# Gate and up of each feed-forward as seven block products instead of eight, with tokens on partitions

## What is computed

```python
def rmsnorm(x, w):                      # over the 1024 features
    return x * rsqrt(mean(x * x, -1) + 1e-6) * w

for l in range(2):
    x = x + 0.5 * (silu(rmsnorm(x, n1) @ w_gate) * (rmsnorm(x, n1) @ w_up)) @ w_down    # feed-forward 0, 2
    x = x + mixed(rmsnorm(x, nm) @ w_in) @ w_out
    x = x + 0.5 * (silu(rmsnorm(x, n2) @ w_gate) * (rmsnorm(x, n2) @ w_up)) @ w_down    # feed-forward 1, 3
x = x + mixed_2(rmsnorm(rmsnorm(x, nf), nm2) @ w_in_2) @ w_o_2
x = x + (silu(rmsnorm(x, n3) @ w_gate_2) * (rmsnorm(x, n3) @ w_up_2)) @ w_down_2        # feed-forward 4
return rmsnorm(x, nf2)
```

## Time and profile before

| | |
|---|---|
| median of 3 runs | 2558.16 us (2556.64 to 2558.29) |
| span of the profiled execution | 2554.3 us; its own time is not among the runs' |
| TensorE busy | 2518.2 us, 11986 matmuls |
| VectorE busy | 1324.1 us |
| ScalarE busy | 567.3 us |
| GpSimd busy | 1519.9 us |
| DMA | 228.67 MB, mean 90 GB/s |
| a feed-forward (1 and 2) | 359.95 and 359.94 us |
| the second block's mixer | 267.72 us |

### The profile page before, as it was taken

The page is one execution under the profiler, slowest core; times in us unless marked ns, Lnnn a source line. Parts: engine busy times, 40 slices in busy tenths (PEclk is TensorE's granted clock), DMA queues, the critical chain, the costliest instruction groups (busy, mean ns, idle before and its releaser), DMA issues.

```text
span 2554.3 us, 33028 instructions
## 1 busy us (share of the span) xinstructions
PE 2518.2 (99%) x11986; PEld 2058.2 (81%) x11986; DVE 1324.1 (52%) x1556; ACT 567.3 (22%) x1033; POOL 1519.9 (60%) x858
## 2 busy tenths in 40 slices
PE   8999999999999999999999999999999988999998
PEld 6888888778888888888888778888887766888887
DVE  6555527656555315556137656555227656655512
ACT  2110014652111001110015552011013564111000
POOL 5666666436666666666665536666664322666664
PEclk9999999999999999999999999999999999999999
DMA  5233222113223223222322113232323111322232
GB/s 169 94 99 99 94 96 75 59 42 98 92 98 99 97 93 99 98 92 98 99 92 74 51 49 99 97 116 98 99 98 134 50 42 34 99 97 93 98 99 74
DMA packets 66724, 228.67 MB, mean 90 GB/s; under 512 B 8784, under 2 KB 11728, under 8 KB 66256
## 3 DMA queue, kind: packets, MB, share of 16 engines
q1 hardware_dynamic: 64928, 225.67, 27.0%
q10 hardware_dynamic: 1712, 1.82, 0.2%
HBM read 225.36 MB, written 2.10 MB: 89 GB/s over the span
## 4 chain that ended last, share of the span: by engine, by line
PE 96%; DVE 2%; ACT 1%; issue 0%; POOL 0%; DMA 0%; SPq 0%; DVEq 0%; POOLq 0%; ACTq 0%
PE bank L610 28%; PE bank L611 28%; PE bank L612 28%; PE bank L627 2%; PE bank L769 2%; PE bank L754 2%; PE bank L738 1%; PE bank L633 1%; PE bank L739 1%; PE bank L992 1%; PE bank L1007 1%; PE bank L984 0%; PE bank L618 0%; PE bank L983 0%; PE bank L899 0%
## 5 line engine op out<-in xcount | busy, mean ns | idle before, releaser
L574 POOL TENSOR_TENSOR wl<-raw,wh 128x1024 fp32r<-128x1024 f32 x412 | 1037.1, 2517 | 34.4
L571 POOL TENSOR_SCALAR wh<-raw 128x1024 fp32r<-128x1024 f32 x412 | 444.8, 1080 | 981.9 <-PE bank L612 944.5
L610 PE MATMUL bank<-xh,wh 128*128 128x512 f32 x2096 | 818.6, 391 | 0.0
L611 PE MATMUL bank<-xl,wh 128*128 128x512 f32 x2096 | 816.4, 389 | 0.0
L612 PE MATMUL bank<-xh,wl 128*128 128x512 f32 x2096 | 816.3, 389 | 0.0
L612 PEld LDWEIGHTS bank<-xh,wl 128*128 128x128 f32 x2096 | 393.5, 188 | 82.7
L610 PEld LDWEIGHTS bank<-xh,wh 128*128 128x128 f32 x2096 | 393.5, 188 | 81.2 <-issue 0.2
L611 PEld LDWEIGHTS bank<-xl,wh 128*128 128x128 f32 x2096 | 393.6, 188 | 81.0 <-issue 0.2
L610 PE MATMUL bank<-acth,wh 128*128 128x512 f32 (+1 forms) x902 | 346.4, 384 | 0.0
L611 PE MATMUL bank<-actl,wh 128*128 128x512 f32 (+1 forms) x902 | 346.2, 384 | 0.0
L612 PE MATMUL bank<-acth,wl 128*128 128x512 f32 (+1 forms) x902 | 346.2, 384 | 0.0
(11 more groups left out here) (273 smaller groups left out, 2352.3 us busy)
## 6 DMA issues: line engine op xcount, KB each, us to landing
raw<-in_stream SPq DMA_DIRECT2D x412, 512.0 KB, 3.6
x<-in_x SPq DMA_DIRECT2D x8, 256.0 KB, 5.9
w1k<-in_w1k SPq DMA_DIRECT2D x1, 2048.0 KB, 9.0
w1v_low<-in_w1v SPq DMA_DIRECT2D x1, 1024.0 KB, 6.7
w1v_high<-in_w1v SPq DMA_DIRECT2D x1, 1024.0 KB, 8.9
out_dram<-x SPq DMA_DIRECT2D x4, 256.0 KB, 2.6
out_dram<-x SPq DMA_DIRECT2D x1, 768.0 KB, 3.7
invcount<-in_c_invcount ACTq DMA_DIRECT2D x1, 512.0 KB, 5.9
```

The costliest lines, as they stand in the source:

```text
L571: nc.gpsimd.tensor_scalar(wh[:, h, :, :], src, 1.0, 1.0, ALU.mult, ALU.mult)\
L574: nc.gpsimd.tensor_tensor(wl[:, h, :, :], src, wh[:, h, :, :].bitcast(F32), ALU.subtract).then_inc(split_done, 1)
L610: mm = nc.tensor.matmul(bank, wh[:, slot, k, :], rh, start=start, stop=False)
L611: mm = nc.tensor.matmul(bank, wh[:, slot, k, :], rl, start=False, stop=False)
```

## The change

Gate and up are computed with tokens on partitions and as a 2x2 block product. A is the normed x without `rstd`, its rows cut into two halves of 256 tokens and its depth into two halves of 512 features. B is, for a chunk of 512 columns of the hidden width, gate beside up: b11 and b21 the two depth halves of gate, b12 and b22 of up. C11 and C21 are gate of the two token halves, C12 and C22 up. The Winograd form has seven block products: A11 b11, A12 b21, S1 T1, S2 T2, S3 T3, S4 b22 and A22 T4, up to signs and names, with four sums of parts of A (made once per feed-forward) and four of B (made per chunk). There are five chunks of 512 columns and a last one of 256, so a full chunk takes 14 half products of 12 matmuls of 512 columns, and the last one 7 products of 24 matmuls of 256 columns.

- The parts of A (`ea`: A11, A12, A22, and `ss`: the four sums) are the stationary operand, the weights the moving one. A half product is two 128-row blocks of B by two tiles of 128 tokens.
- Weights come as four loads of 1 MB per chunk (b11, b12, b21, b22) into five buffers of which one holds t1; sums of B are written over the raw operands. ScalarE makes the high part of each half product's weights (`high_weights`, 128x1024), VectorE the sums (`sum_weights`, 8 per chunk of 128x1024) and the low parts (`low_weights`, 14 per chunk of 128x1024). They go round three slots: the two of the unit stream and `wx`. GpSimd does nothing for gate and up; for feed-forward 0 it makes the scaled copy `xg` of x.
- At the end of each product ScalarE copies (`first_copy`, `second_copy`, `third_copy`) and VectorE combines (`gate_first`, `up_second`, `up_first`) partial results out of PSUM, times `rc` or `nrc`, 1/rms of a token as a column. The mean comes from four matmuls with one column each (`token_sums_of`). Silu follows (`first_silu`, `second_silu`), then gate x up (`rows_first`, `rows_second`).
- The hidden tiles then have tokens on partitions. `act_turn` turns tile f with four float32 transposes into bank 6 or 7, ScalarE copies the high part (`high_act`), VectorE takes the low part (`low_act`). Eight of the 22 are turned between the last chunk's products 3 to 6, two after them, and twelve between the blocks of the first output tile of down.
- Down, the mixers and the last norm stay, but for their buffers' places; loops over units on TensorE, ScalarE, VectorE and SP, and most on GpSimd, are written out. The unit stream has 192 units. Some semaphores are merged.

The core of the diff (`PREP[n]` is the number of the seam; `DOWN_AT[n]` the first unit of down; on ScalarE and VectorE, `feed_forward` and `seam` have the same name):

```diff
+OPERAND = ("b11", "b21", "b11", "t1", "b12", "b22", "b21")
+SUM_OF = {2: 1, 3: 0, 4: 2, 6: 3}
...
+            def first_chunk(n):
+                if n in (1, 3):
+                    sp.wait_ge(ml_done, (n // 2) * 8 + 9)
+                if n == 2:
+                    sp.wait_ge(unit_used, DOWN_AT[1] + 20 + 3)
+                if n == 4:
+                    sp.wait_ge(mh2_done, 8)
+                for role in ("b11", "b12", "b22"):
+                    load_quarter(n, 0, role)
+                sp.wait_ge(split_done, DOWN_AT[n] - (2 if n == 2 else 0))
+                load_quarter(n, 0, "b21")
...
+            def next_chunk(n, c):
+                for role, i in (("b11", 3), ("b12", 4), ("b21", 5), ("b22", 6)):
+                    sp.wait_ge(gu_lo, product_end(n, c - 1, i))
+                    load_quarter(n, c, role)
...
+            def product(n, c, i):
...
+                if i == 4:
+                    pe.wait_ge(copied, (n * CHUNKS + c) * 6 + 4)
...
+                banks = third_banks if i in (3, 5) else second_banks(c) if i == 1 else first_banks(c)
+                w = width(c)
+                for half in range(halves_of(c)):
+                    g = part(c, i, half)
+                    wh_, wl_ = high_slot(slot_of(n, g)), low_slot(slot_of(n, g))
+                    pe.wait_ge(gu_lo, n * GU + g + 1)
+                    for at in range(4 // halves_of(c)):
+                        k = 2 * half + at
+                        if c == 0 and i < 2:
+                            pe.wait_ge(a_lo, n * 12 + 4 * i + k + 1)
+                        r = slice(at * w, at * w + w)
+                        for t in range(2):
+                            m = slice(t * P, t * P + P)
+                            if i in (0, 1, 6):
+                                sh, sl = ea[:, i % 5 + i // 6, 0, k, m], ea[:, i % 5 + i // 6, 1, k, m]
+                            else:
+                                sh, sl = ss[:, i - 2, 0, k, m], ss[:, i - 2, 1, k, m]
+                            o = B[banks[t]][:, 0:w]
+                            first, final = k == 0 and i in (0, 1, 3), k == 3
+                            nc.tensor.matmul(o, sh, wh_[:, r], start=first, stop=False, skip_group_check=True)
+                            nc.tensor.matmul(o, sl, wh_[:, r], start=False, stop=False, skip_group_check=True)
+                            mm = nc.tensor.matmul(o, sh, wl_[:, r], start=False, stop=final, skip_group_check=True)
+                    mm.then_inc(gu_used, 1)
...
+            def token_sums_of(n):
+                pe.wait_ge(ones_in, 16)
+                pe.wait_ge(sq_used, PREP[n] * 8 + 12)
+                for i in range(NQ):
+                    mm = nc.tensor.matmul(B[7][:, i:i + 1], rstd[:, i * P:(i + 1) * P], ones[:, 0:1], start=True, stop=True)
+                mm.then_inc(ss_done, 1)
...
+            def act_turn(n, f):
+                c = f // 4
+                pe.wait_ge(p_done, (n * CHUNKS + c) * 4 + 4)
+                if f >= 2:
+                    pe.wait_ge(act_done, n * FT + f - 1)
+                for t in range(NQ):
+                    tr = nc.tensor.transpose(B[6 + f % 2][:, t * P:(t + 1) * P],
+                                             product_rows(c)[:, t, (f % 4) * P:(f % 4) * P + P], ident[:, :])
+                tr.then_inc(t_act, 1)
...
+                for c in range(CHUNKS):
+                    for i in range(7):
+                        product(n, c, i)
+                        if c == 0 and i == 0:
+                            token_sums_of(n)
+                        if c == LAST and i >= 3:
+                            if i == 3 and n == 0:
+                                pe.wait_ge(const_in, 16 * N_CONST)
+                            act_turn(n, 2 * i - 6)
+                            act_turn(n, 2 * i - 5)
+                act_turn(n, 8)
+                act_turn(n, 9)
...
+                        if m == 0 and f + 10 < FT:
+                            act_turn(n, f + 10)
...
+                for i in range(7):
+                    if i < 5:
+                        high_weights(n, LAST, i + 2, 0)
+                    if i == 0:
+                        second_silu(n, LAST - 1)
+                    if i == 1:
+                        first_copy(n, LAST)
+                    if i == 3:
+                        second_copy(n, LAST)
+                    if i == 4:
+                        third_copy(n, LAST)
+                        first_silu(n, LAST)
+                    if i >= 5:
+                        high_act(n, 2 * i - 10)
+                        high_act(n, 2 * i - 9)
+                high_act(n, 4)
+                high_act(n, 5)
+                second_silu(n, LAST)
+                for f in range(6, FT):
+                    high_act(n, f)
...
+            def seam(n, g):
+                for m in range(KT):
+                    if n != 2 and m == 6:
+                        high_weights(n, 0, 0, 0)
+                        high_weights(n, 0, 0, 1)
+                    if n == 2 and m == 7:
+                        high_weights(n, 0, 0, 0)
+                        high_weights(n, 0, 0, 1)
+                    if m == 7:
+                        high_weights(n, 0, 1, 0)
+                    tile_parts(n, m, g(m))
...
+            def low_weights(n, c, i, half):
+                g = part(c, i, half)
+                slot = slot_of(n, g)
+                dve.wait_ge(gu_hi, n * GU + g + 1)
+                V.tensor_tensor(low_slot(slot), buffered(c, OPERAND[i], half), high_slot(slot).bitcast(F32), ALU.subtract)\
+                    .then_inc(gu_lo, 1)
...
+            def up_second(n, c):
+                dve.wait_ge(gu_used, product_end(n, c, 4))
+                dve.wait_ge(copied, (n * CHUNKS + c) * 6 + 6)
+                for t in range(2):
+                    e = sq[:, 2 + t, 0:width(c)]
+                    V.scalar_tensor_tensor(e, B[first_banks(c)[t]][:, 0:width(c)], nrc[:, 2 + t:3 + t], e, ALU.mult, ALU.add)\
+                        .then_inc(combined, 1)
...
+            def low_act(n, f):
+                dve.wait_ge(acth_done, n * FT + f + 1)
+                V.tensor_tensor(actl(f), B[6 + f % 2][:, :], acth(f).bitcast(F32), ALU.subtract).then_inc(act_done, 1)
...
+                for c in range(LAST):
+                    for h in range(QUARTERS):
+                        if c == 0:
+                            if h == 1:
+                                token_mean(n)
+                                if n in (0, 2):
+                                    sum_weights(n, 0, 0, 0)
+                                    sum_weights(n, 0, 0, 1)
+                                sum_weights(n, 0, 1, 0)
+                            if h == 2:
+                                low_sum(n, 0)
+                                token_scale(n)
+                            if h == 3:
+                                sum_weights(n, 0, 1, 1)
+                                sum_rows(n, 2)
+                            if h == 4:
+                                low_sum(n, 1)
+                                sum_rows(n, 3)
+                            if h == 5:
+                                low_sum(n, 2)
+                            if h == 7:
+                                low_sum(n, 3)
+                        else:
+                            if h == 0:
+                                rows_first(n, c - 1)
+                            if h == 1:
+                                sum_weights(n, c, 1, 0)
+                            if h == 2:
+                                sum_weights(n, c, 1, 1)
+                            if h == 3:
+                                rows_second(n, c - 1)
+                        if h in (4, 5):
+                            sum_weights(n, c, 2, h - 4)
+                        if h == 6:
+                            gate_first(n, c)
+                        if h in (7, 8):
+                            sum_weights(n, c, 3, h - 7)
+                        if h == 10:
+                            up_second(n, c)
+                        if h in (11, 12) and (c < LAST - 1 or h == 11):
+                            sum_weights(n, c + 1, 0, h - 11)
+                        if h == 13:
+                            up_first(n, c)
+                            if c == LAST - 1:
+                                sum_weights(n, LAST, 1)
+                        if (c, h) != (0, 0):
+                            low_at(n, c, h + 2)
+                for i in range(7):
+                    if i == 0:
+                        sum_weights(n, LAST, 2)
...
+                for i in range(7):
+                    if i == 0:
+                        sum_weights(n, LAST, 2)
+                        rows_first(n, LAST - 1)
+                    if i == 1:
+                        sum_weights(n, LAST, 3)
+                        rows_second(n, LAST - 1)
+                    if i == 2:
+                        gate_first(n, LAST)
+                    if i == 5:
```

(28 more changed lines are left out.)

751 lines of the change are left out of this document (505 added, 246 removed).

## The result

The changed kernel takes 2618.7 us (median; 2618.1 to 2619.6) where the kernel before takes 2557.4 (2556.2 to 2558.3): 1.0241 times as long, 95% interval 1.0227 to 1.0256. The prediction was 2543 with a range of 2490 to 2572 and 0.60 for faster: the sign is wrong and the time lies outside the range, 76 us above the forecast. The profiled execution has a span of 2616.4 us.

The account below looks back on a forecast made before the run. TensorE, busy 99% of the span, was taken as the bound. The 2554.3 us span less 98.3 of matmul work plus 41, 15.6, 13.9 and 13.3 of waits gave 2539.8; with 3.9 for the median, 2543, range 2490 to 2572.

Parts of the forecast that it names:

- the sum: Whole kernel: span 2554.3 less 98.3 of TensorE work plus 41, 15.6, 13.9 and 13.3 of waits, giving 2539.8 us.
- rival (a): Tails of gate and up: TensorE's clock falls to half, costing 5 us per tail, 2568 us in all; chance 0.17.
- 340.3 us of work in a feed-forward, 98.3 less in all: TensorE in each feed-forward: 340.3 us of work against 359.95, 19.65 less each, 98.3 over five.
- VectorE keeps up: Full chunks of gate and up: VectorE needs 31.4 us, some 33 with waits, under TensorE's 38.1.
- Rival (c): Chunks of gate and up: VectorE bound at 1.5 us an instruction, 2.4 us over per chunk, 2603 us; chance 0.08.
- The tail, 8.2 us, five times, 41: End of gate and up: TensorE waits for transposed tiles through two banks, 8.2 us per feed-forward, 41 in all.
- the walk: Stepping through the engines' queues in order to predict TensorE's waits at tails, seams and start, such as half product 10 at 53.9.
- Seams: Start of feed-forwards: token sums and first chunk wait, 5.2 us each for 1, 3 and 4, 13.9 for 2.
- Rival (b): Tails and seams: the waits hide, tails cost 2 us and seams 2, total 2495 us; chance 0.18.
- (d): Chunks of gate and up: loads or instruction fetch stall them by 1 us or more, 2568 us and up; chance 0.07.
- the 2.4 that the prediction has there: Seam of feed-forward 2: 2.4 us lost before product 0, with loads that overlay down's buffers.

Follow-up runs that it names:

- e10: The changed kernel with 480 unused bytes a partition allocated behind nrc: 2578.0 us, 1.0079 of the kernel before.
- e8: e5 with the same instructions in another queue order in the tail of gate and up: 2546.6 us, 0.9954 of the kernel before.
- e5: The changed kernel with one unused tensor of 32 bytes a partition behind nrc: 2602.4 us, 1.0172 of the kernel before.
- e11: e10 with e8's tail order and three more small changes of order: 2516.8 us, 0.9841 of the kernel before.
- e9: Separate TensorE-only kernel, operands 0 to 480 bytes apart modulo 512: 0.2267 us a matmul at distance 0, 0.2333 at 32.
- e6: The kernel before with 32 unused bytes a partition behind room: 2576.7 us, 1.0074 of the kernel before.
- e7: The kernel before with 32 unused bytes a partition ahead of all its tensors: 2557.7 us, 0.9997 of the kernel before.

## Why the prediction was wrong

**The step that failed** is in the sum: "Of the changes left, moving `rstd` to a column, shorter reciprocals, other buffers and unrolled loops lie on engines under TensorE; I put them at nothing." Buffers don't lie on an engine; they are what TensorE reads.
**The distance isn't the whole miss.** e10 takes 2578.0 us: above the top of the range (2572), and 20 us more than before where a gain was forecast. The second step that failed is that the sum has no term for the clock: every matmul in it goes at full speed, and half clock stands only in rival (a), with a chance of 0.17. e10's span is 2576.2, the predicted one 2539.8: 36.4 us. Its mixers take 230.92, 230.95 and 267.75 us, as before, so the 36.4 lie in the feed-forwards and the end. Counted from the starts in both traces:

- Waits: 92.6 by the view of waits (43.2 + 20.4 + 17.2 + 6.0 + 3.9 + 1.9), less before's own 8.8, so 83.8 are new, and 83.8 were foreseen. That the sum fits is luck in its parts: the tails cost 43.2 for 41, the wait for `second_silu` 6.0 for nothing, start and seams 34.6 for 42.8.
- Half clock: what starts on TensorE while the granted clock is 0.50 takes 21.7 us more than at full clock, in the same stretches of before 3.1. That is 18.6.
- The matmul ahead of a wait: the view counts a wait from the end of that matmul, the sum counts the matmul as 0.2267 and it lasts 0.39. 46 such matmuls against 3 in before cost 6.7 us.
- About 11 are not assigned; they lie thinly over many matmuls.

Point by point:
- *340.3 us of work in a feed-forward, 98.3 less in all*: nearly right once distance and clock are. Feed-forward 1 of e10 takes 361.5 us; without its waits, its half clock and the matmuls ahead of waits 342.7 are left. In e10 a full chunk takes 38.08 us (the copy of the first product starts at 702.94, 741.02 and 779.10), predicted 38.1. The transposes of the tails take 48.1 us, predicted 48, and that is luck: in e8, where none runs at half clock, the 440 take 41.7, 0.095 each for the 0.109 of the sum.
- *VectorE keeps up*: right. The row of the 1024-element instruction that the trace of before didn't have (from the kernel after), and the window of one full chunk in e10, TensorE busy all of it, VectorE 32.62 us (predicted 31.4, some 33 with waits):

```profile
L2036 DVE TENSOR_TENSOR wl<-rawa,wh 128x1024 fp32r<-128x1024 f32 x155 | 189.3, 1223 | 82.5 <-ACT wh L1454 82.5
```

```profile
698.10:736.20 38.10, 38.10 (x170) 31.56 (x169) 32.62 (x33) 20.54 (x26) 0.00 (x0) 1.00 0.31 111
```

  Back to back their starts are 1.14 apart, estimated 1.15; the 1.39 from which VectorE would be the bound is far. Rival (c) is out.
- *The tail, 8.2 us, five times, 41*: 43.2 in 20 waits, for the reason given, as e8 shows. Its parts were less right than its sum: the four waits were 1.9, 2.7, 2.5 and 1.1 in the prediction and are 1.66, 4.73, 1.36 and 0.90 in e5's timeline, the second one longer because `rows_first`, a VectorE instruction with two SBUF inputs, ran beside GpSimd's split of down's first weights, 2.96 us for two instead of the 0.84 by the earlier trace rows; the walk missed it here though it had priced it in `rows_second`. The rows of the kernel after:

```profile
848.41 2.96 DVE L2086 TENSOR_TENSOR plast<-plast,sq 128x256 f32<-128x256 f32 x2
...
848.71 2.38 POOL L729 TENSOR_TENSOR wl<-raw,wh 128x1024 fp32r<-128x1024 f32 x1
```

- *Seams*: token sums 0.9 (feed-forwards 1 and 3), 5.3 (2) and 3.7 (4), and 8.2 in feed-forward 0; predicted 1.4 for 1, 3 and 4, and 5.5 for 2. The 5.5 was right in size and cause (e11 takes it away). Feed-forward 0 of e10 ends at 383.49, where the prediction has 372.92 - 19.65 + 8.2 + 13.3 = 374.8. Its half product 10 starts at 57.24 where the walk has 53.9, 3.3 of the difference: the token sums come at 27.85, not 26, and they and the nine matmuls behind them go at half clock, which the walk left out. (So do the first twelve, but the wait for the token sums covers that.) The rest comes later, 1.5 by the wait below and 1 to 2 by the tail's half clock.
- *Not seen*: the wait of product 1 of the last chunk for `second_silu`, 1.5 us in four feed-forwards, 6.1.
- *Rival (a)*, the clock falls in the tails, happened in all five tails, at the 4.7 us wait. It costs 11.7 us there by e5 and e8 (8.1 + 3.6), half of the 25 that the rival asked; the rest of the 18.6 is at seams and start, where the rival didn't look. The Trainium skill ("TensorE: Matmul & The Clock Gate", section "Part 4: PE-mode transpose") says that transposes don't count as busy in the way matmuls do, which would make the fall more likely. No run tests that by itself. e8 has the same 440 transposes, and with the 4.7 us waits gone the clock falls in no tail, so they alone don't bring the fall; whether they help the wait to bring it is open. Rival (b) is out, the waits didn't hide. Of (d) there is nothing: the one `issue` wait of 1.6 us, ahead of feed-forward 2's first product, ends where VectorE's low part of that weight does (992.55 in the kernel after), behind ScalarE's wait for the load; it is the 2.4 that the prediction has there. Rival (b) was also mispriced: 2 us a seam takes 42.8 down to 10, which is 33 and not 17, and 2479 would have been outside the range.

So the counts of the change were worked out rightly, the waits in their sum, and the forecast was still wrong by 76 us: 41 from an input that was taken over instead of asked, whether the pace belongs to the instruction or also to its addresses, and 19 from the clock, which was seen as a rival and left out of the sum.

## What to carry to other kernels

Before a matmul's pace is carried over from one kernel to another, compare the distances between the starts of the two operands, not only the shapes; a small tensor added between them can shift one against the other, and 3% on a kernel that TensorE bounds is more than most changes bring. If untouched stages change their pace after an edit, look at what they share with it, addresses first. And a wait on TensorE can cost more than itself, because the work behind it runs at half clock, here in every tail at a wait of 4.7 us and at some seams behind one of 1 us; give it a term in the sum. Order the in-order queues so that what TensorE needs next stands ahead of evacuations that nobody waits for.

## What the runs showed of the hardware

- A stream of fp32r matmuls, 128 by 128 against 512 columns, starts one every 0.2267 us when the two SBUF operands start a multiple of 256 bytes apart, 0.229 when the moving one starts 64 bytes past such a distance from the stationary one, and 0.2325 to 0.2342 at the other multiples of 32 (e9, one execution, no other engine at work). Behind a switch of the distance the first matmuls keep a slower pace: five in the kernel after, seven in e6, one or two in e9. The common shift of both does nothing (e7). Kernels: 18 us for 32 bytes (e6), 40.7 for 480 (e10).
- The small f32 matmuls of the mixers, as the 16 that take 1.88 us in the chain, had the same time in the kernel after and in e10.
- At a wait of 4.73 us the granted clock fell to 0.50 and stayed there 3 to 5 us behind the wait (the kernel after, five tails; up to 6 in e5). Behind the wait of 1.66 us in the same tails it stayed at 1.00, and behind one of 1.05 us at the seam of feed-forward 1, followed by eight one-column matmuls, it fell for 3.4 us (e5, e8). In the same place of e11, behind a wait of 1.19 us, it fell at the seam of feed-forward 3 and not at that of feed-forward 1.
- VectorE with two SBUF inputs: 1024 elements alone 1.22 us, starts 1.14 apart; 256 elements beside a GpSimd split 1.48 us.
